# The second experts' gather on one Trainium2 core: the first expert's columns apart, the rest within its up product, ring slots in the order of use

## What is computed

```python
D_MODEL, SEQ, N_EXPERTS_2, TOP_K_2, FFN_EXPERT = 1024, 256, 8, 2, 1408

def _swiglu(h, wg, wu, wd):
    return (jax.nn.silu(h @ wg) * (h @ wu)) @ wd

def _moe(h, router, wg, wu, wd):
    b, s, d = h.shape
    hf = h.reshape(b * s, d)
    probs = jax.nn.softmax((hf @ router).astype(F32), axis=-1)
    top_p, top_i = lax.top_k(probs, TOP_K_2)
    top_p = top_p / jnp.sum(top_p, -1, keepdims=True)
    gates = jnp.sum(jax.nn.one_hot(top_i, N_EXPERTS_2, dtype=F32) * top_p[..., None], axis=1)
    out = jnp.zeros_like(hf)
    for e in range(N_EXPERTS_2):
        out = out + gates[:, e:e + 1] * _swiglu(hf, wg[e], wu[e], wd[e])
    return out.reshape(b, s, d)
```

## Time and profile before

| | us |
|---|---|
| median of three runs | 2812.84 |
| lowest and highest run | 2811.42, 2815.39 |
| profiled execution | 2811.0 |
| its span | 2809.2 |
| TensorE busy in the span | 2597.4 (92%) |
| second experts, from the first load's issue to TensorE's last down product | 2407.0 to 2793.5 |

### The profile page before, as it was taken

The page is one execution under the profiler, slowest core; times in us unless marked ns, Lnnn a source line. Parts: engine busy times, 40 slices in busy tenths (PEclk is TensorE's granted clock), DMA queues, the critical chain, the costliest instruction groups (busy, mean ns, idle before and its releaser), DMA issues.

```text
span 2809.2 us, 38587 instructions
## 1 busy us (share of the span) xinstructions
PE 2597.4 (92%) x15511; PEld 1540.8 (55%) x15511; DVE 867.1 (31%) x1612; ACT 520.3 (19%) x1063; POOL 369.9 (13%) x486
## 2 busy tenths in 40 slices
PE   7999999998999989999898789999999999899996
PEld 4446766687333423334333258787887787743442
DVE  4666155312211111111121025451011546312223
ACT  2111122301221211112121122321001333300001
POOL 2010234100110111101011100221020011000000
PEclk9999899999999999999999889999999999899998
DMA  7334320237999999999999952127533301569997
GB/s 256 128 141 163 114 91 30 96 144 286 381 419 420 419 420 419 420 420 418 421 419 419 420 218 90 61 74 262 172 134 103 119 31 61 225 268 424 424 423 305
DMA packets 165304, 720.37 MB, mean 256 GB/s; under 512 B 13076, under 2 KB 42352, under 8 KB 103552
## 3 DMA queue, kind: packets, MB, share of 16 engines
q1 hardware_dynamic: 158576, 699.44, 62.6%
q0 software_dynamic: 6144, 18.24, 1.7%
q10 hardware_dynamic: 400, 0.15, 0.0%
HBM read 705.07 MB, written 12.71 MB: 256 GB/s over the span
## 4 chain that ended last, share of the span: by engine, by line
PE 68%; SPq 14%; DMA 9%; DVE 4%; issue 2%; ACT 1%; POOL 0%; PEldq 0%; DVEq 0%; ACTq 0%; POOLq 0%
PE P L776 67%; SPq L742 13%; DMA R<-in_w_gate_up 3%; DMA R<-in_moe_w_up 2%; DVE R L1808 2%; PE P L779 2%; DMA R<-in_moe_w_gate 1%; DMA R<-in_w_down 1%; DMA R<-in_moe_w_down 1%; DMA WS<-in_w_gate_up 1%; ACT R L2690 1%; DVE R L1814 1%; SPq L707 1%; SPq L726 1%; DMA WS<-in_w_mod 0%
## 5 line engine op out<-in xcount | busy, mean ns | idle before, releaser
L776 PE MATMUL P<-R 128*32 128x256 f32 (+11 forms) x7632 | 1042.5, 435 | 97.3 <-DMA R<-in_w_down 25.8
L776 PEld LDWEIGHTS P<-R 128*32 128x32 f32 (+5 forms) x7632 | 514.8, 145 | 590.9 <-issue 423.8
L2690 ACT ACTIVATE R<-P 128x512 f32<-128x512 f32 (+3 forms) x412 | 199.8, 490 | 1767.4 <-PE P L776 1415.9
L776 PE MATMUL P<-R,WS 128*128 128x256 f32 (+1 forms) x1888 | 507.3, 427 | 7.2 <-ACT R L2690 3.0
L776 PE MATMUL P<-WS,R 128*32 128x256 f32 (+5 forms) x2764 | 459.5, 498 | 31.8 <-DMA WS<-in_w_gate_up 11.9
L776 PEld LDWEIGHTS P<-R,WS 128*128 128x128 f32 x1888 | 357.8, 192 | 140.5 <-issue 96.1
L776 PE MATMUL P<-xT,WS 128*128 128x256 f32 (+2 forms) x1728 | 400.1, 385 | 9.3 <-ACT xT L2690 3.5
L776 PEld LDWEIGHTS P<-xT,WS 128*128 128x128 f32 (+2 forms) x1728 | 317.4, 188 | 70.8 <-issue 20.9
L776 PEld LDWEIGHTS P<-WS,R 128*64 128x64 f32 (+2 forms) x2764 | 174.1, 135 | 273.8 <-issue 210.4
L1808 DVE TENSOR_TENSOR R<-P,R 128x512 f32<-128x512 f32 (+2 forms) x158 | 88.5, 574 | 564.5 <-PE P L776 471.3
L3240 POOL PARTITION_BROADCAST R<-R x180 | 121.0, 672 | 703.9 <-DMA R<-in_b_gate_up 344.0
(11 more groups left out here) (207 smaller groups left out, 876.8 us busy)
## 6 DMA issues: line engine op xcount, KB each, us to landing
R<-in_w_gate_up SPq DMA_DIRECT2D x167, 1024.0 KB, 26.5
WS<-in_w_gate_up SPq DMA_DIRECT2D x89, 1024.0 KB, 26.6
R<-in_w_down SPq DMA_DIRECT2D x85, 1024.0 KB, 26.4
WS<-in_w_in SPq DMA_DIRECT2D x60, 1024.0 KB, 7.4
WS<-in_w_down SPq DMA_DIRECT2D x43, 1024.0 KB, 26.6
R<-in_moe_w_gate SPq DMA_DIRECT2D x24, 1408.0 KB, 20.2
WS<-in_w_mod SPq DMA_DIRECT2D x24, 1024.0 KB, 7.6
R<-in_moe_w_up SPq DMA_DIRECT2D x16, 1408.0 KB, 27.4
```

The source lines that it names most:

```text
L776: return nc.tensor.matmul(out, lhsT, rhs, start=start, stop=stop, skip_group_check=True)
L2690: return nc.scalar.activation(out, in_, f, **kw)
```

## The change

It does five things.

1. `first_columns`: from the ranks alone (`KW2`, now the first product of `slots`), VectorE makes `G0`, the one-hot tile of expert 0's 96 columns (`one_hot` 1), and TensorE gathers them with 16 products of 128x96 into banks 4 to 7. ScalarE copies them straight into `XG2[:, 0]` (`turned`, `turn_free`). GpSimd's `columns(0)` is gone.
2. The eight jobs `xm` stand between the two pairs of up 0, in two banks in turn (6 and 7), with ScalarE's copies after its sigmoid of gate 0. `Gs1` is ready with `one_hot` 2 and 3, `Gw2` with 5.
3. `MSLOT` follows use: load n takes the slot of the load that is used as the (n-10)th. The first ten are set by hand.
4. `RANK` puts rank 5 (a narrow expert) in place 1 and rank 1 in place 2.
5. In wide products the second pair does the parts with 32 first, then those with 64 (`parts`), and a wide product waits for both loads of a pair ahead of it.

```diff
-RANK = [0, 1, 5, 2, 3, 4, 6, 7]
+RANK = [0, 5, 1, 2, 3, 4, 6, 7]
...
-MSLOT = [n % MRING for n in range(90)] + [2, 3, 4, 5, 6, 7]
+MTURN = [(x, kind, s) for x, kind in MORDER for s in range(4)]
+MSLOT = [4, 5, 2, 3, 0, 1, 6, 7, 8, 9]
+for _n in range(MRING, 96):
+    MSLOT.append(MSLOT[MNTH[MTURN[_n - MRING + (2 if _n >= 90 else 0)]]])
...
+            def first_columns():
+                pe.wait_ge(S("one_hot"), 1)
+                for i in range(4):
+                    b = P[4 + i]
+                    for kk in range(2):
+                        for c in range(2):
+                            last = mm(b[:, CAP0 * kk:CAP0 * kk + CAP0], xrow[:, c, 2 * i + kk::KT], G0[:, c, :], c == 0, c == 1)
+                    last.then_inc(S("turned"), 1)
...
                     for s0 in (0, 2):
-                        w = {}
-                        for s in (s0, s0 + 1):
-                            w[s] = loaded((x, kind, s))
+                        w = {s: loaded((x, kind, s)) for s in (s0, s0 + 1)} if wide(x) else {}
+
+                        def low(s):
+                            w[s] = loaded((x, kind, s)) if s not in w else w[s]
                             for k in (2 * s, 2 * s + 1):
+                                if x == 0 and kind == "gate" and k in (0, 2):
+                                    pe.wait_ge(S("turn_free"), 28 + k // 2 + 1)
...
+                        if x == 0 and kind == "gate" and s0:
+                            pe.wait_ge(S("turn_free"), 28 + 4)
+                        if x == 0 and kind == "up" and s0:
+                            for i in range(8):
+                                place(job("xm", i), i // 4 + 2, i % 4, xrow, Gs1)
+                        parts = (low,) if not wide(x) else (high, low) if s0 else (low, high)
+                        for part in parts:
+                            for s in (s0, s0 + 1):
+                                last = part(s)
+                                if part is parts[-1]:
+                                    used(last, x, kind, s)
...
                 if l:
                     router(1, 8, xk)
-                    for i in range(8):
-                        place(job("xm", i), i // 4 + 1, i % 4, xrow, Gs1)
+                    first_columns()
                 empty_all()
...
                 cnt, start = cnt0[:, 0:ne], start0[:, 0:ne]
+                V(tt(KW2[:, 0:2, :], b[:, 0:2 * ne].rearrange("p (c e) -> p c e", c=2), msk))
+                dve.wait_ge(S("pool_set"), 3)
+                for c in range(2):
+                    ins = ts(G0[:, c, :], iota2[:, 0:CAP0], KW2[:, c, 0:1], None, ALU.is_equal, ALU.bypass)
+                    if c:
+                        mark(ins, "one_hot")
...
                     if x:
                         out_(x - 1)
                     else:
+                        for i in range(8):
+                            n, b = ready("xm", i)
+                            p, q = i % 4, i // 4
+                            F(n, fn(XSm[:, 2 * p:2 * p + 2, 256 * q:256 * q + 256],
+                                    b[:, :].rearrange("p (k n) -> p k n", k=2), ACT.Copy))
+                        for c in range(2):
+                            mark(fn(xrow[:, c, :], xrow[:, c, :], ACT.Identity, scale=ALPHA), "scalar_step")
...
-                    for i in range(8):
-                        n, b = ready("xm", i)
-                        p, q = i % 4, i // 4
-                        F(n, fn(XSm[:, 2 * p:2 * p + 2, 256 * q:256 * q + 256], b[:, :].rearrange("p (k n) -> p k n", k=2), ACT.Copy))
-                    for c in range(2):
-                        mark(fn(xrow[:, c, :], xrow[:, c, :], ACT.Identity, scale=ALPHA), "scalar_step")
+                    for i in range(4):
+                        act_.wait_ge(S("turned"), 28 + i + 1)
+                        fn(XG2[:, 0, 2 * i:2 * i + 2, :], P[4 + i][:, 0:2 * CAP0].rearrange("p (k n) -> p k n", k=2), ACT.Copy)                            .then_inc(S("turn_free"), 1)
...
                 pool.wait_ge(S("cnt_ready"), 2)
-                pool.wait_ge(S("mm_free"), START["xm"] + 4)
-                columns(0)
                 pool.wait_ge(S("mm_free"), START["xm"] + 8)
                 columns(1)
```

## The result

| | before | changed |
|---|---|---|
| median | 2814.25 us (5 runs) | 2797.53 us (5 runs) |
| lowest, highest | 2811.42, 2816.17 | 2794.77, 2802.11 |
| profiled execution, its span | 2811.0, 2809.2 | 2796.47, 2794.8 |

The ratio is 0.9944 with an interval of 0.9933 to 0.9955: 15.8 us faster, between 12.7 and 18.9. The forecast was 2795, that is 18.0 us less than before, in a range of 2790 to 2803; the time lies in it. The trace of each kernel is of one execution, so that its numbers are of one execution too.

What follows compares the result with a forecast made beforehand. The end of the weight transfers was taken as the bound, set by load 18's start. Its 18.0 us took the profiled 2811.0 to 2793.0; the median's 1.8 above that gave 2795, range 2790 to 2803.

Steps and rivals of the forecast that it cites:

- Load 18: Weight load of expert 1's up part 2, counted from 0; claimed to start at 2490.3 instead of 2508.3, 18.0 us earlier.
- The slot is what held it: Load 18 waited for the slot of expert 0's down part 0; its new slot is expert 1's gate part 0.
- Rival 3: Load 18 still waits for the first slot of expert 0's down product; gain 5.2 us, 2807.6; chance 4%.
- The start of the gather: TensorE's gather of the first columns claimed to start at 2433.3, after one small product and two VectorE compares.
- The price of the first gather: 32 records at 0.218 each, 7.0 us at half clock throughout; claimed end 2440.0, bounds 2438.4 and 2445.4.
- the same 5.8 from 2433.3: TensorE's clock claimed to rise 5.8 us after the first gather's start, at 2439.1, speeding its last quarter.
- three signs of being wrong: A half clock beyond 2443, a TensorE wait between 2484 and 2496, or a hole in the transfers after 2490.
- The sum: TensorE's chain from the first gather: load 16 moves from 2483.4, expert 1's gate product starts at 2485.5, load 18 at 2490.3.
- Loads 18 to 95 go without a gap: Weight transfers from load 18 to the last claimed to run without a hole, at 421 GB/s.
- The saving goes to the end in full: Transfers still set the end, so load 18's 18.0 us come off the whole time: 2811.0 to 2793.0.
- Costed at nothing: Scatter weights on VectorE and GpSimd (1.8 at least left), expert 0's transposes, waits for both loads, table entries: no cost.
- TensorE's slack: TensorE alone would end at 2769.0, the transfers let it end at 2775.5: 6.5 us to spare.

Runs made afterwards that it cites:

- e1: The kernel before with the new slot table and the new ranks alone, gather in its old place; ratio to before 0.9939.
- e4: The kernel before with the new slot table alone, old ranks; ratio to before 0.9955.
- e5: e1 with products of constants where TensorE waits (7 ahead of the router, 1 ahead of ranking, 5 behind it); ratio to before 0.9925.
- e2: The whole change with the old slot table and old ranks, leaving the gather in two pieces and the part order; ratio to before 1.0004.
- e3: The whole change with the old slot table alone; ratio to before 0.9988.
- e8: The whole change with 12 products of constants (5.1 us) ahead of expert 3's down product; one run, 2797.18 us.
- e9: The whole change with 30 products of constants (12.8 us) ahead of expert 3's down product; one run, 2805.16 us.
- e11: The whole change with products of constants ahead of the router (7) and the ranking products (1); ratio to before 0.9938.
- e6: e1 with the change's order of parts in wide products and its waits for both loads of a pair; ratio to before 0.9926.
- e7: The whole change, but the gather of the first expert's columns multiplies 256 columns instead of 96; ratio to before 0.9940.
- e10: Slots, ranks, order of parts and e5's products of constants, gather of all columns in its old place; ratio to before 0.9914, median 2790.41 us.

## Why the prediction was right, and where not

**Load 18 as the one question.** Right, and shown: e1, e4 and e5 move its start and the end follows; e2 moves everything ahead of it and nothing follows.

**The slot is what held it; the ranks are worth 2.4 at it.** Right. (The ranks came to 3.1 by R to end.) Rival 3, slots without effect, was priced at 5.2 us of gain; e3 is that case, measured by R to end at 3.9 and by the ratio at 3.4.

**The start of the gather.** It was put at 0.95 after R and came at 1.35, 0.4 later. The two compares of 128x96 took 0.98 together; in e2 the same two took 0.58, and there the gather did start 0.95 after R. The traces differ in what GpSimd does at that time. In the changed kernel its fill of 128x768 runs from 2434.34 to 2435.10, beside the compares (start us, us, engine, line):

```profile
2434.34 0.76 POOL L3453 MEMSET R<- 128x768 f32 x1
```

```profile
2434.50 0.98 DVE L1849 TENSOR_SCALAR R<-R,small 128x96 f32<-128x96 f32 x2
```

In e2 it is over when they begin:

```profile
2432.92 0.76 POOL L3449 MEMSET R<- 128x768 f32 x1
```

```profile
2433.69 0.58 DVE L1845 TENSOR_SCALAR R<-R,small 128x96 f32<-128x96 f32 x2
```

e3, e8 and e9 are as e2 (0.57 to 0.58, the fill over), e11 as the changed kernel (0.98, the fill beside them). So in six traces the compares take 0.4 us more just where the fill falls on them. The two slow ones are also the two in which TensorE's clock was up at that time, and that is why they meet the fill: the ranking products end sooner against it. The clock alone isn't the reason, as VectorE's compares of 128x256 take 0.35 at either clock (before at half, e5 at full). All this is read from traces that happened to differ, and no run moved the fill to test it.

**The price of the first gather: this step failed.** 0.218 a record was 0.238 (7.9 us instead of 6.7), well inside the bounds. (By the prediction's own prices the 6.7 should have been 6.4: 5.8 us at half clock make 26.6 records, and the other 5.4 take 0.6 at full.) Of the Trainium skill's rule ("TensorE: Matmul & The Clock Gate", Part 3, "What overlaps and what doesn't"), that a weight load overlaps products in flight only in other row groups, the trace says that it doesn't hold here: 0.238 is far from the sum of load and columns, which I had put at 0.378. But "the same 5.8 from 2433.3" was wrong: I took the time to the clock's rise from products of 256 columns and gave it to products of 96. It was 9.9 us, and gate 0 took 15.5 us instead of 14.8. A half clock beyond 2443 was one of the three signs of being wrong, and it came: to 2445.4, or 2443.6 counted with R where it was before. The router could have warned: TensorE was busy with products of 8 columns for 6.97 us and the clock stayed at 0.50.

**The sum.** Predicted from R: load 16 at 51.0, gate 1 at 53.1, load 18 at 57.9. Measured: 53.8, 55.7, 60.7. The 2.8 that load 16 was late are 0.4 of the gather's start, 1.2 of the gather, 0.7 of gate 0 and 0.4 of the gather of all columns (15.6 instead of 15.2), to 0.1. So load 18 came 15.2 us earlier, not 18.0. The end gained 16.5, for another 1.3 that I hadn't looked for: in the 20 us from load 18's start the transfers moved 375 GB/s before and 415 in the changed kernel (423 later on), 1.9 us of transfers; the 0.6 that this is too much isn't explained. Part of the 1.9 is the pause between load 19 and load 20 before, which then too waited for down 0. "Loads 18 to 95 go without a gap" wasn't quite so in the kernel before, and that the total came as near to the forecast as 16.5 to 18.0 is in part luck: without this it would have been 15.2. "The saving goes to the end in full" was right.

**Costed at nothing.** VectorE's four compares and the three operations of gate 0 ended at 2488.7, 1.2 ahead of gate 1; TensorE has no wait between 2481.9 and 2513.9. Right, with 0.6 us less slack than I had. The order of parts was priced as no loss; it saves 0.3 us a wide product.

**TensorE's slack.** Predicted 6.5 us; the waits and the half clock in the trace come to 12. The 0.3 us of each of the 13 wide products from expert 1 on would be 4 of the difference. e9 shows that the number alone says little.

**What the forecast missed.** It priced the sum of five edits and not each against the rest. The working holds the finding: gate 1 starts at 2485.5 "(before: 2485.65)". The gather in two pieces bought nothing at the one place that counts, and the words didn't say so. In the traces it costs 1.7 us there.

## What to carry to other kernels

Where a ring of buffers feeds an engine and loads and uses have different orders, a slot table by load number makes a load wait for a buffer that is used late; a table by order of use has the same loads and products and was worth 13.6 us here. When a change has several parts, ask of each what it moves at the one event that sets the end: two holes in the transfers looked alike in the profile, and closing the first alone was worth nothing. A hole in a saturated resource is only worth what comes out at its last restart.

## What the runs showed of the hardware

- TensorE can be busy without a break while its granted clock stays at 0.50, or falls. With products of 128x256 that began at 0.50 and behind a wait, it rose 5.0 to 5.8 us after their start in five kernels (before, e1, e4, e6, e7). With products of 128x96, it had not risen in their 7.9 us in any of five (whole, e2, e3, e8, e9), and rose 9.2 to 12.5 us after their start, in the products behind them. In e5 it fell from 1.00 to 0.50 2.7 us after the start of the router's products of 128x8, with TensorE busy for 5.8 us until then; in e11 about 1.0 us after the start of the gather of 96, behind a wait of 1.35, and in the whole change 0.3 us before that start, in the same wait.
- The same instructions met another clock in another execution: the router took 5.45 us in the trace of the whole change and 6.97 in those of e2, e3, e8 and e9.
- Products that nobody reads, put where TensorE waits, shortened the traces: 13 of them by 4.8 us in e5 against e1 (2.9 ahead of R, 1.9 behind it), and by the ratios 3.9 us, with intervals that overlap. In e10, which has them beside the slots, the ranks and the order of parts, the interval (0.9899 to 0.9929) is clear of that of the whole change (0.9933 to 0.9955).
- VectorE's compares of 128x96 took 0.98 us a pair with a fill on GpSimd beside them (two traces), and 0.57 to 0.58 without (four).
- Products with 32 and with 64 columns of weights, put in the order 64, 32, 32, 64 instead of 64, 32, 64, 32, took 14.5 instead of 14.8 us for the same 128 records.
